# Beta's logarithm in the decay's bias, and the recurrence's dense products in one run of six, in the gated delta rule of a two-block model

## The chip, the cores and the metric

One core of one Trainium2 chip runs the whole program. The time is the device time of one execution in microseconds. The kernel before takes 2220.82 us (median of 3 runs, 2219.01 to 2222.67). The profiled execution took 2220.63 us.

## What the kernel computes

Two residual blocks run over 512 tokens of width 1024. The first has two layers: a gated delta rule mixer and a latent attention mixer, each followed by a SwiGLU. The second has a windowed attention and retention mixer, a convolution mixer and two cross attentions to a memory of 256 tokens. The change lies in the gated delta rule alone. Cut to what matters, for each of 8 heads (128 wide):

```python
beta = sigmoid(b_in);  g = -exp(a_log) * softplus(a_in + dt_bias)
kb = k * beta[..., None]
decay = exp(where(tril, g_cum_i - g_cum_j, -inf))
L = where(strict, einsum("id,jd->ij", kb, k) * decay, 0)
A = L + eye
u = triangular_solve(A, v * beta[..., None])
w = triangular_solve(A, kb * exp(g_cum)[..., None])
attn = einsum("id,jd->ij", q, k) * decay
# recurrence over the chunks:
v_new = u - w @ S
o = (q * exp(g_cum)) @ S + attn @ v_new
S = S * exp(g_last) + (k * exp(g_last - g_cum)).T @ v_new
```

followed by a norm of o, a gate silu(gate), and the output product with `gdn_w_out`.

## The kernel before, in words

**Engines.** The program is written by hand, one instruction list for each engine, and the engines meet in semaphores. SyncE (SP) loads the weights in slabs of 128 columns. GpSimd (POOL) splits each slab in two instructions into a high and a low part: `wH` (line 568) and `wL` (line 570). A split waits until the slab three places earlier has been used up (`slab_done`). TensorE (PE) forms each dense product as three products, high by high, high by low and low by high. ScalarE (ACT) does copies, exponentials and SiLU, and VectorE (DVE) the rest.

**A head.** The 8 heads of the delta rule run one after another in `head(i, ahead)` (PE line 924, ACT 1736, DVE 2337). Tokens are taken in four chunks of 128. While PE works on head i it also forms the four projections of head i+1 (key, query, value, gate: 96 dense products of 512 columns, `head_units`, line 826), dealt out in runs between the small products of head i: `dense(n)` issues the next n. In the last head, 7, there is no next head (`ahead` is false), and products of the memory's keys and values (`kv0`, `kv1`, 24 products of 256 columns to a slab) and of the output projection (`gdn_out`, `out_third`) take that place.

A head has three parts:

- *Opening.* ACT makes the logarithm and powers of the keys' squared norms (lines 1715 to 1718), squares the previous head's output (`head_squares`, line 1702) and exponentiates the decay with a bias for each key, `dec_bias` (line 1725). DVE adds the query norm's term to those squares (`head_sums`, line 2319), and PE sums them with a product by ones (line 922), whose result ACT turns into the norm (1707, 1709). PE forms the keys by (keys times beta) (line 939) and keys by queries (line 952). DVE multiplies the first by the decay (`LT`, line 2342) and starts the inverse of A in blocks of 64 (lines 2347 and 2350).
- *Inversion.* Five rounds of 64 by 64 products (line 901) with `dense(4)` between them. Each round passes through DVE.
- *Recurrence.* For each chunk t: values by inverse (line 1009), w by S (1013, which waits for the new state S), S by queries (1016), a dense run of four, the state's increment (1024) and the output (1025), a dense run of two. ACT copies `v_new` (1765). DVE updates S (2408, 2411), then filters a row of the next head's value (`conv`, 2291), then forms one row sum of the modulation weights (`ada_row`, 2082, 128x1024), which belongs to a later layer.

**Rows over tokens.** `head_rows` (line 840) spreads two rows of head i+1 over 128 partitions, each by one product from 64 partitions: the decay's sums behind t = 1, and beta behind t = 3. DVE multiplies the keys by the spread beta (`keys_by_beta`, line 2304), which the product of line 939 waits for. `key_factors` (2309 to 2313) makes the three small factors `dec_bias`, `kdec_by` and `v_by`.

## Time and profile before

| what | value |
|---|---|
| median of 3 runs | 2220.82 us |
| profiled execution, own time | 2220.63 us |
| its span | 2218.8 us |
| PE busy | 2151.1 us (97%) |
| DVE busy | 1152.6 us (52%) |
| ACT busy | 604.3 us (27%) |
| POOL busy | 1218.5 us (55%) |
| PE's share of the chain that ended last | 88% |

The 1.8 us between the span and the execution's own time lie around the first and the last instruction. The eight heads lie between about 75 and 450 us of the span. In the timeline a PE instruction's start is what counts: the products are pipelined, so that durations overlap, and a dense product of 512 columns starts some 0.23 us behind the one before it. A product in full fp32 is shown as two instructions (x2 for one product).

### The profile page before, as it was taken

To read this page: it belongs to the slowest core of one execution; us is meant where nothing else is said; L and a number is where in the kernel's file an instruction comes from. 1 tells how busy PE (TensorE), PEld (TensorE's weight loads), DVE (VectorE), ACT (ScalarE), POOL (GpSimd) and SP (SyncE) were. 2 spreads that over 40 slices of the span, in tenths; PEclk is the share of its full clock that TensorE was granted. 3 is DMA by queue.
4 is the path that set the end of the run, shared out by engine and by line. 5 is a ranking of instruction groups with operands and counts; after the bars stand their busy time and mean duration, and the time that the engine had idled before them with its cause. 6 is when DMAs were issued, how large, how long until landed. Compare 5 with 4: busy or idle time off the path is not lost.

```text
span 2218.8 us, 29386 instructions
## 1 busy us (share of the span) xinstructions
PE 2151.1 (97%) x11960; PEld 1716.1 (77%) x11960; DVE 1152.6 (52%) x1595; ACT 604.3 (27%) x1234; POOL 1218.5 (55%) x687
## 2 busy tenths in 40 slices
PE   7899999989999999999999999999999999999998
PEld 5677777778888887777788888777777878887886
DVE  4666666557457374554431322477764365346332
ACT  4434543332112023342320201422332230002113
POOL 5433333367778676333566666554445276657663
PEclk9999999999999999999999999999999999999999
DMA  8522322246465453111333333322224133333331
GB/s 272 174 75 88 105 68 87 77 143 207 144 199 180 152 185 106 58 52 49 114 101 99 95 95 94 97 80 73 67 58 123 39 114 98 96 91 95 105 105 66
DMA packets 366020, 239.88 MB, mean 108 GB/s; under 512 B 11352, under 2 KB 350654, under 8 KB 365759
## 3 DMA queue, kind: packets, MB, share of 16 engines
q1 hardware_dynamic: 364268, 234.07, 35.1%
q10 hardware_dynamic: 1618, 3.94, 0.5%
q8 instruction: 95, 1.56, 0.3%
q14 instruction: 39, 0.31, 0.0%
HBM read 233.79 MB, written 4.19 MB: 107 GB/s over the span
## 4 chain that ended last, share of the span: by engine, by line
PE 88%; DVE 5%; POOL 2%; ACT 2%; DMA 1%; issue 1%; SPq 1%; ACTq 0%; DVEq 0%; POOLq 0%
PE bank L611 16%; PE bank L613 16%; PE bank L612 16%; PE bank L835 8%; PE bank L630 3%; PE bank L632 3%; PE bank L631 3%; PE mid L901 2%; POOL wL L570 1%; PE mid L1408 1%; PE bank L647 1%; PE bank L649 1%; PE bank L648 1%; PE bank L868 1%; DVE WIDE L2082 1%
## 5 line engine op out<-in xcount | busy, mean ns | idle before, releaser
L568 POOL TENSOR_SCALAR wH<-stage 128x1024 fp32r<-128x1024 f32 (+1 forms) x340 | 387.3, 1139 | 944.8 <-PE bank L613 260.3
L570 POOL TENSOR_TENSOR wL<-stage,wH 128x1024 fp32r<-128x1024 f32 (+1 forms) x340 | 831.9, 2447 | 28.4
L611 PE MATMUL bank<-hH,wH 128*128 128x512 f32 x944 | 368.6, 390 | 0.7 <-DVE A L2159 0.3
L613 PE MATMUL bank<-hH,wL 128*128 128x512 f32 x944 | 367.4, 389 | 0.0
L612 PE MATMUL bank<-hL,wH 128*128 128x512 f32 x944 | 367.3, 389 | 0.0
L611 PE MATMUL bank<-RA,wH 128*128 128x512 f32 (+1 forms) x788 | 284.6, 361 | 7.6 <-DVE RA L2173 3.0
L612 PE MATMUL bank<-RA,wH 128*128 128x512 f32 (+1 forms) x788 | 282.4, 358 | 0.0
L613 PE MATMUL bank<-RA,wL 128*128 128x512 f32 (+1 forms) x788 | 282.3, 358 | 0.0
L611 PEld LDWEIGHTS bank<-hH,wH 128*128 128x128 f32 x944 | 177.2, 188 | 39.7 <-issue 3.3
L613 PEld LDWEIGHTS bank<-hH,wL 128*128 128x128 f32 x944 | 177.2, 188 | 37.0
L612 PEld LDWEIGHTS bank<-hL,wH 128*128 128x128 f32 x944 | 177.2, 188 | 36.7 <-issue 0.2
L611 PEld LDWEIGHTS bank<-RA,wH 128*128 128x128 f32 x788 | 150.0, 190 | 32.6 <-issue 5.2
L612 PEld LDWEIGHTS bank<-RA,wH 128*128 128x128 f32 x788 | 150.2, 191 | 21.8 <-issue 0.5
L613 PEld LDWEIGHTS bank<-RA,wL 128*128 128x128 f32 x788 | 150.2, 191 | 21.4
L2082 DVE CUSTOM_DVE_ANT_0 WIDE<-WIDE,cbc,vec 128x1024 f32<-128x1024 f32 x80 | 158.4, 2009 | 0.7 <-DMA WIDE<-in_ada_t 0.6
L1561 ACT ACTIVATE A<-bank 128x512 f32<-128x512 f32 (+1 forms) x85 | 47.0, 556 | 374.6 <-PE bank L613 354.5
L2142 DVE SCALAR_TENSOR_TENSOR xT<-bank,modT,xT 128x512 f32<-128x512 f32 x62 | 46.5, 751 | 177.9 <-PE bank L613 167.8
L630 PE MATMUL bank<-hH,wH 128*128 128x512 f32 x296 | 128.7, 435 | 6.4 <-POOL wL L570 6.1
L2211 DVE TENSOR_TENSOR A<-bank,A 128x512 f32<-128x512 f32 x44 | 30.4, 692 | 196.4 <-PE bank L613 190.8
L632 PE MATMUL bank<-hH,wL 128*128 128x512 f32 x296 | 116.6, 394 | 0.0
L631 PE MATMUL bank<-hL,wH 128*128 128x512 f32 x296 | 116.1, 392 | 0.0
L835 PE MATMUL bank<-hL,wH 128*128 128x512 f32 x248 | 108.0, 435 | 0.0
(418 smaller groups left out, 3526.5 us busy)
## 6 DMA issues: line engine op xcount, KB each, us to landing
WIDE<-in_ada_t SPq DMA_DIRECT2D x46, 1024.0 KB, 6.1
stage<-in_ffn_w_gate SPq DMA_DIRECT2D x44, 512.0 KB, 3.8
stage<-in_ffn_w_up SPq DMA_DIRECT2D x44, 512.0 KB, 3.8
stage<-in_c_wkv SPq DMA_DIRECT2D x32, 512.0 KB, 3.9
stage<-in_gdn_w_in SPq DMA_DIRECT2D x32, 512.0 KB, 4.1
stage<-in_ffn_w_down SPq DMA_DIRECT2D x32, 512.0 KB, 3.9
stage<-in_o_w_in SPq DMA_DIRECT2D x32, 512.0 KB, 4.0
stage<-in_e_w_in SPq DMA_DIRECT2D x26, 512.0 KB, 3.8
```

Of the source, the lines that this page charges most:

```text
L568: pool.tensor_scalar(high[:, 0:n], raw[:, 0:n], 1.0, 0.0, ALU.mult, ALU.add).then_inc(w_high, 1)
L570: pool.tensor_tensor(low[:, 0:n], raw[:, 0:n], high[:, 0:n].bitcast(F32), ALU.subtract).then_inc(w_split, 1)
L611: pe.matmul(bank[:, 0:n], h[:, k, c], xh[:, k, :], start=first and k == 0, stop=False)
L612: pe.matmul(bank[:, 0:n], h[:, k, c], xl[:, k, :], start=False, stop=False)
L613: mm = pe.matmul(bank[:, 0:n], l[:, k, c], xh[:, k, :], start=False, stop=last and k == kc - 1)
L630: pe.matmul(acc[j % 2][:], h, hH[:, k, :], start=k == 0, stop=False)
L631: pe.matmul(acc[j % 2][:], h, hL[:, k, :], start=False, stop=False)
L632: mm = pe.matmul(acc[j % 2][:], l, hH[:, k, :], start=False, stop=k == KD - 1)
L835: mm = pe.matmul(acc[j % 2][:], l if part == 2 else h, (hL if part == 1 else hH)[:, k, :], start=k == 0 and part == 0, stop=k == KD - 1 an ...
L1561: act.activation(out, acc[b][:, 0:n], func).then_inc(taken[b], 1)
L2082: ins = dve.tensor_tensor_reduce(out=w, in0=w, in1=c_bank if n < ADA_HEAD else cbc[:], scale=1.0, scalar=vec[:, at:at + 1], op0=ALU.mult, ...
L2142: dve.scalar_tensor_tensor(out=xT[:, k, :], in0=bank[:], scalar=gate[:, k:k + 1], in1=xT[:, k, :], op0=ALU.mult, op1=ALU.add).then_inc(tak ...
```

## The change

Beta leaves the rows. Its logarithm, minus ln(1 + exp(-b)), is taken up in `tok[:, 0]`, so that `dec_bias` carries it, and the decay that DVE multiplies by is already scaled by beta of the key's token. So one row instead of two is made and spread (`head_row`), `keys_by_beta` and `v_by` go, and the product of keys by keys needs the keys alone. It moves from the opening into the recurrence of the head before, at t = 1 (`keys_by_keys`). Keys by queries takes its place in the opening, goes to bank B5 instead of B4, and no longer waits for the norm of the head before. The product by ones follows it directly.

In the recurrence `dense(4)` and `dense(2)` become one `dense(6)` ahead of the wait for `v_new`, and the first `ada_row` of a head moves from behind the first state into the last round of the inversion. In the last head the 48 products of `kv1` are dealt out in runs of six beside the rounds (`beside`), the output projection follows later, and 12 products instead of 3 stand behind the product by ones of head 7.

**PE, recurrence, t = 1 into t = 2, head 1.** Before (L1016 is S by queries, L1024 and L1025 the increment and the output, L848 the spread row, L1009 and L1013 the next chunk's first two):

```order
L1016 MATMUL mid<-A,S 128x128
L835 MATMUL bank1<-hL,wH1 128x512
L835 MATMUL bank1<-hH,wL1 128x512
L835 MATMUL bank1<-hH,wH1 128x512
L835 MATMUL bank1<-hL,wH1 128x512
L1024 MATMUL mid<-A 128x128
L1025 MATMUL mid<-A 128x128
L835 MATMUL bank1<-hH,wL1 128x512
L835 MATMUL bank1<-hH,wH1 128x512
L848 MATMUL mid<-RA,pick 128x512
L1009 MATMUL mid<-A 128x128
L1013 MATMUL mid<-S,A 128x128
```

After (the same products are now L1037, L1049, L1050, L845 and L1030; L854 is keys by keys, and L834 the dense product):

```order
L1037 MATMUL mid<-A,S 128x128
L854 MATMUL mid<-A 128x128 x4
L834 MATMUL bank1<-hL,wH1 128x512
L834 MATMUL bank1<-hH,wL1 128x512
L834 MATMUL bank1<-hH,wH1 128x512
L834 MATMUL bank1<-hL,wH1 128x512
L834 MATMUL bank1<-hH,wL1 128x512
L834 MATMUL bank1<-hH,wH1 128x512
L1049 MATMUL mid<-A 128x128
L1050 MATMUL mid<-A 128x128
L845 MATMUL mid<-RA,pick 128x512
L1030 MATMUL mid<-A 128x128
```

Keys by keys stands ahead of the dense run, and the two runs are one: nothing dense is left between the increment and the next chunk.

**PE, opening of head 2.** Before (L939 is keys by beta's keys, L922 the product by ones, L952 keys by queries):

```order
L835 MATMUL bank0<-hL,wH2 128x512
L939 MATMUL mid<-A 128x128 x4
L835 MATMUL bank0<-hH,wL2 128x512
L835 MATMUL bank0<-hH,wH2 128x512
L922 MATMUL mid<-A,tab 128x512
L835 MATMUL bank0<-hL,wH2 128x512
L835 MATMUL bank0<-hH,wL2 128x512
L835 MATMUL bank0<-hH,wH2 128x512
L835 MATMUL bank0<-hL,wH2 128x512
L835 MATMUL bank0<-hH,wL2 128x512
L835 MATMUL bank0<-hH,wH2 128x512
L952 MATMUL mid<-A 128x128 x4
```

After (L968 is keys by queries, L942 the product by ones, L921 what L901 was):

```order
L834 MATMUL bank0<-hL,wH2 128x512
L968 MATMUL mid<-A 128x128 x4
L942 MATMUL mid<-A,tab 128x512
L834 MATMUL bank0<-hH,wL2 128x512
L834 MATMUL bank0<-hH,wH2 128x512
L834 MATMUL bank0<-hL,wH2 128x512
L834 MATMUL bank0<-hH,wL2 128x512
L834 MATMUL bank0<-hH,wH2 128x512
L834 MATMUL bank0<-hL,wH2 128x512
L834 MATMUL bank0<-hH,wL2 128x512
L834 MATMUL bank0<-hH,wH2 128x512
L921 MATMUL mid<-tab,inv 64x64 x8
```

The product by ones now stands eight dense products behind the head's start where it stood ten, and the 64 by 64 products follow its eight dense ones directly.

**DVE, end of head 2 and opening of head 3.** Before (L2298 is the decay's row, L2304 `keys_by_beta`, L2309 to L2313 `key_factors`, L2319 `head_sums`, L2342 the product that makes `LT`):

```order
L2291 SCALAR_TENSOR_TENSOR yt<-bank,cw,yt 128x509
L2082 ISA WIDE,modT<-WIDE,cbc,vec 128x1024
L2082 ISA modT 128x1
L2298 TENSOR_TENSOR A<-mid,tab 128x512
L2304 TENSOR_TENSOR A<-mid,A 128x512
L2309 SCALAR_TENSOR_TENSOR kn<-kn,tok 128x4
L2312 TENSOR_TENSOR kn<-kn,tok 128x4
L2313 TENSOR_TENSOR kn<-kn,tok 128x4
L2319 SCALAR_TENSOR_TENSOR A<-sq,A 128x512
L2342 TENSOR_TENSOR A<-mid,A 128x512
L2347 TENSOR_TENSOR inv<-A,tab 64x2x64 x4
```

After (L2326 is the decay's row, L2331 and L2334 `key_factors`, L2340 `head_sums`, L2363 makes `LT`):

```order
L2319 SCALAR_TENSOR_TENSOR yt<-bank,cw,yt 128x509
L2110 ISA WIDE,modT<-WIDE,cbc,vec 128x1024
L2110 ISA modT 128x1
L2326 TENSOR_TENSOR A<-mid,tab 128x512
L2331 SCALAR_TENSOR_TENSOR kn<-kn,tok 128x4
L2334 TENSOR_TENSOR kn<-kn,tok 128x4
L2340 SCALAR_TENSOR_TENSOR A<-sq,A 128x512
L2363 TENSOR_TENSOR A<-mid,A 128x512
L2368 TENSOR_TENSOR inv<-A,tab 64x2x64 x4
```

Two instructions are gone ahead of `head_sums`; the order of the rest stands.

The diff, without the declarations:

```diff
--- before.py
+++ after.py
...
@@ -815,9 +815,8 @@
                 pe.matmul(B4[:, 32:64], ones, gflat, start=True, stop=True).then_inc(g["gsum"], 1)
-                for bank, n, by in ((SS, 4, table("upto")), (B5, 1, ident)):
-                    for t in range(TT):
-                        mm = pe.matmul(bank[0:8, t * P:(t + 1) * P], tok[:, n, t, :], by, start=True, stop=True)
+                for t in range(TT):
+                    mm = pe.matmul(SS[0:8, t * P:(t + 1) * P], tok[:, 4, t, :], table("upto"), start=True, stop=True)
                 mm.then_inc(g["gsum"], 1)
@@ -837,16 +836,37 @@
 
-            def head_rows(i, n):
+            def head_row(i):
 
                 if i == 0:
-                    pe.wait_ge(g["rowlo"], 2)
-                elif n == 0:
+                    pe.wait_ge(g["rowlo"], 1)
+                else:
                     pe.wait_ge(g["p"], i * 6)
-                else:
-                    pe.wait_ge(g["s"], i * 3)
-                pe.matmul((SS, B5)[n][:], pick[0:64, i:i + 1].broadcast_to((64, P)), gate_row[:, n, :],
+                pe.matmul(SS[:], pick[0:64, i:i + 1].broadcast_to((64, P)), gate_row,
                           start=True, stop=True).then_inc(g["rows"], 1)
+
+            def keys_by_keys(i):
+
+                if i:
+                    pe.wait_ge(g["wt"], i)
+                for t in range(TT):
+                    c = slice(t * P, (t + 1) * P)
+                    mm = pe.matmul(B3[:, c], k_[:, c], k_[:, c], start=True, stop=True)
+                mm.then_inc(g["gram"], 1)
+
+            def kv_units(name, j, first, end):
+
+                s, uses = SLAB0[name] + j, USE0[name] // 2 + j // 2
+                for n in range(first, end):
+                    k, part = divmod(n, 3)
+                    if n == 0:
+                        pe.wait_ge(w_split, s + 1)
+                        free(j % 2, uses)
+                    h, l = (w[:, k, :] for w in halves(s))
+                    mm = pe.matmul(acc[j % 2][:, 0:MEM], l if part == 2 else h, (memL if part == 1 else memH)[:, k, :],
+                                   start=n == 0, stop=n == 3 * KD - 1)
+                    if n == 3 * KD - 1:
+                        mm.then_inc(slab_done, 1)
 
@@ -925,6 +945,13 @@
 
+                def beside(n):
+
+                    if n < 8:
+                        kv_units("kv1", n // 4, n % 4 * 6, n % 4 * 6 + 6)
+                    else:
+                        gdn_out((n - 8) // 2, (n % 2,))
+
                 def dense(n):
@@ -932,40 +959,32 @@
                 if not ahead:
-                    kv_slabs("kv0", (0,))
-                pe.wait_ge(g["kb"], i + 1)
+                    kv_units("kv0", 0, 0, 3 * KD)
+                pe.wait_ge(g["silu"], i * 3 + 2)
+                if i:
+                    pe.wait_ge(g["s"], i * 3)
                 for t in range(TT):
                     c = slice(t * P, (t + 1) * P)
-                    mm = pe.matmul(B3[:, c], k_[:, c], Pm[:, c], start=True, stop=True)
+                    mm = pe.matmul(B5[:, c], k_[:, c], q[:, c], start=True, stop=True)
                 mm.then_inc(g["gram"], 1)
-                at = dense(2)
                 if i:
                     head_squares(i - 1)
-                at = dense(6)
+                at = dense(8)
                 if not ahead:
-                    kv_slabs("kv0", (1,))
-                pe.wait_ge(g["silu"], i * 3 + 2)
-                if i:
-                    pe.wait_ge(g["ors"], i)
-                for t in range(TT):
-                    c = slice(t * P, (t + 1) * P)
-                    mm = pe.matmul(B4[:, c], k_[:, c], q[:, c], start=True, stop=True)
-                mm.then_inc(g["gram"], 1)
-                if not ahead:
-                    kv_slabs("kv1", (0,))
+                    kv_units("kv0", 1, 0, 3 * KD)
 
...
                 if not ahead:
-                    kv_slabs("kv1", (1,))
+                    beside(0)
                 for n in range(1, 6):
...
                     if not ahead:
-                        gdn_out(n - 1, (0,))
+                        beside(2 * n - 1)
                     if n == 1 and i:
@@ -978,7 +997,7 @@
                     if not ahead:
-                        gdn_out(n - 1, (1,))
+                        beside(2 * n)
 
@@ -986,7 +1005,8 @@
                 if not ahead:
-                    gdn_out(5)
+                    gdn_out(1, (1,))
+                    gdn_out(2, (0,))
                 pe.wait_ge(g["p"], i * 6 + 6)
@@ -994,7 +1014,8 @@
                 if not ahead:
-                    gdn_out(6)
+                    gdn_out(2, (1,))
+                    gdn_out(3)
 
@@ -1014,22 +1035,23 @@
                         pe.matmul(B6[:, c], S[:, t % 2, :], E[:, c], start=True, stop=False)
+                        if ahead and t == 1:
+                            keys_by_keys(i + 1)
                     elif ahead:
                         keys_turn(i + 1)
-                    at = dense(4)
-                    if not ahead:
-                        out_third("gdn_out", t, t, t + 1)
+                    at = dense(6)
+                    if not ahead and t < TT - 1:
+                        gdn_out(4 + t)
+                    elif not ahead:
+                        out_third("gdn_out", 0, 0, 1)
                     pe.wait_ge(g["vn"], i * 4 + t + 1)
...
                         mm.then_inc(g["o_ps"], 1)
-                    at = dense(2)
                     if ahead and t == 1:
-                        head_rows(i + 1, 0)
-                    if ahead and t == TT - 1:
-                        head_rows(i + 1, 1)
+                        head_row(i + 1)
                 at = dense(2)
@@ -1038,15 +1060,16 @@
             keys_turn(0)
-            head_rows(0, 0)
-            head_rows(0, 1)
+            head_row(0)
+            keys_by_keys(0)
             for i in range(0, 7):
...
             head(7, False)
-            for k in range(4, 6):
+            for k in range(1, 3):
                 out_third("gdn_out", k, k, k + 1)
             head_squares(7)
-            out_third("gdn_out", 6, 6, 7)
+            for k in range(3, 7):
+                out_third("gdn_out", k, k, k + 1)
             gdn_out(7)
@@ -1719,7 +1742,7 @@
                 act.wait_ge(g["dec"], i + 1)
-                act.wait_ge(g["kds"], 3 * i + 1)
+                act.wait_ge(g["kds"], 2 * i + 1)
                 for t in range(TT):
@@ -1729,8 +1752,9 @@
                 copy_sum(1, SLAB0["gdn"] + i * 4 + 3, gs[i % 2])
-                act.wait_ge(g["kds"], 3 * i + 3)
+                act.wait_ge(g["kds"], 2 * i + 2)
                 scaled_tiles(kdec, B7, lambda t: kdec_by[:, t:t + 1]).then_inc(g["tok"], 1)
+                act.wait_ge(g["gexp"], 2)
                 scaled_tiles(ktok, B7, lambda t: tok[:, 2, t, i:i + 1]).then_inc(g["tok"], 1)
@@ -1742,16 +1766,19 @@
                     head_sum(i + 1, 0)
-                else:
-                    kv_copies(1)
                 if i:
...
                 act.activation(gs[i % 2], gs[i % 2], ACT.Silu).then_inc(g["gs"], 1)
+                if not ahead:
+                    kv_copies(1, (0,))
                 act.wait_ge(g["vtr"], i + 1)
-                scaled_tiles(v, B7, lambda t: v_by[:, t:t + 1]).then_inc(g["v"], 1)
+                act.wait_ge(g["rk"], 3 * i + 3)
+                scaled_tiles(v, B7, lambda t: k_norm[:, t:t + 1]).then_inc(g["v"], 1)
+                if not ahead:
+                    kv_copies(1, (1,))
                 if ahead:
@@ -1777,6 +1804,8 @@
             act.activation(tmp8[:, 0], tmp8[:, 3], ACT.Exp, scale=-1.0).then_inc(g["eb"], 1)
+            act.wait_ge(g["eb"], 1)
+            own(act.activation(tmp8[:, 3], tmp8[:, 0], ACT.Ln, bias=1.0))
             act.wait_ge(par_in, 64)
@@ -1786,13 +1815,12 @@
             gc = B4[:, 0:32].rearrange("p (t h) -> p t h", h=8)
-            act.activation(tmp8[:, 0], gc, ACT.Exp).then_inc(g["gexp"], 1)
+            act.activation(tok[:, 2], gc, ACT.Exp).then_inc(g["gexp"], 1)
             act.wait_ge(g["zab"], 2)
...
             act.wait_ge(g["pick"], 1)
-            for n, bank in enumerate((SS, B5)):
-                act.activation(gate_row[0:8, n, :], bank[0:8, :], ACT.Copy).then_inc(g["rowhi"], 1)
+            act.activation(gate_row[0:8, :], SS[0:8, :], ACT.Copy).then_inc(g["rowhi"], 1)
             act.preload_act_table_set(SILU)
@@ -2294,23 +2322,16 @@
 
-                dve.wait_ge(g["rows"], i * 2 + 1)
+                dve.wait_ge(g["rows"], i + 1)
                 dve.tensor_tensor(tiles(decs[i % 2]), tiles(SS[:]), on_tiles(table("decay_neg")), ALU.add).then_inc(g["dec"], 1)
-
-            def keys_by_beta(i):
-
-                dve.wait_ge(g["rows"], i * 2 + 2)
-                dve.wait_ge(g["silu"], i * 3 + 1)
-                dve.tensor_tensor(Pm, B5[:], k_, ALU.mult).then_inc(g["kb"], 1)
 
...
                                          op0=ALU.mult, op1=ALU.subtract).then_inc(g["kds"], 1)
-                dve.wait_ge(g["rk"], 3 * i + 3)
+                dve.wait_ge(g["rk"], 3 * i + 2)
                 dve.tensor_tensor(kdec_by, k_inv2, tok[:, 3, :, i], ALU.mult).then_inc(g["kds"], 1)
-                dve.tensor_tensor(v_by, k_norm, tok[:, 1, :, i], ALU.mult).then_inc(g["kds"], 1)
 
@@ -2351,7 +2372,7 @@
                 dve.wait_ge(g["gram"], i * 2 + 2)
-                own(dve.tensor_tensor(attn, B4[:], dec, ALU.mult))
+                own(dve.tensor_tensor(attn, B5[:], dec, ALU.mult))
                 own.settle()
@@ -2395,6 +2416,7 @@
                         dve.sem_inc(g["xt"], 1)
+                        ada_row(3 * i)
                     below(n)
@@ -2413,10 +2435,10 @@
                         conv(i + 1, 2, (2 - t,))
-                    ada_row(3 * i + t)
+                    if t:
+                        ada_row(3 * i + t)
                 if ahead:
                     decay_rows(i + 1)
-                    keys_by_beta(i + 1)
                     key_factors(i + 1)
@@ -2454,18 +2476,17 @@
                .then_inc(g["zab"], 2)
+            dve.wait_ge(g["zab"], 2)
+            own(dve.tensor_tensor(tok[:, 0], tok[:, 0], tmp8[:, 3], ALU.add))
             dve.wait_ge(g["gexp"], 2)
-            own(dve.tensor_tensor(tok[:, 2], tok[:, 1], tmp8[:, 0], ALU.mult))
+            own(dve.tensor_tensor(tok[:, 3], tok[:, 3], tok[:, 1], ALU.mult))
             dve.wait_ge(kv_out, 16 * 2)
...
             own.settle()
-            for n, bank in enumerate((SS, B5)):
-                dve.wait_ge(g["rowhi"], n + 1)
-                dve.tensor_tensor(gate_row[32:40, n, :], bank[0:8, :], gate_row[0:8, n, :].bitcast(F32), ALU.subtract)\
-                   .then_inc(g["rowlo"], 1)
+            dve.wait_ge(g["rowhi"], 1)
+            dve.tensor_tensor(gate_row[32:40, :], SS[0:8, :], gate_row[0:8, :].bitcast(F32), ALU.subtract).then_inc(g["rowlo"], 1)
             conv(0, 2, (2, 1, 0))
             decay_rows(0)
-            keys_by_beta(0)
             key_factors(0)
...
                 head(i, True)
```

## Rows read from the trace of the kernel before

**Rows 1.** Windows view: us, busy us of PE, PEld, DVE, ACT, POOL, clock, DMA share, GB/s.
```profile
75.00:450.00 375.00, 365.51 (x3602) 278.56 (x3600) 237.65 (x455) 160.39 (x421) 129.05 (x72) 1.00 0.29 86
...
403.50:407.00 3.50, 3.50 (x17) 3.50 (x18) 2.28 (x5) 2.19 (x9) 1.05 (x1) 0.52 0.54 159
```

**Rows 2.** Timeline, PE, head 3's recurrence: start us, us, engine line op, tiles, count.
```profile
260.41 0.40 PE L835 MATMUL bank<-hH,wH 128*128 128x512 f32 x1
...
261.16 0.49 PE L1009 MATMUL mid<-A 128*128 128x128 f32 x2
262.10 0.46 PE L1013 MATMUL mid<-S,A 128*128 128x128 f32 x2 [0.45 <-DVE S L2411]
```

**Rows 3.** Timeline, DVE, end of the inversion and the recurrence, head 3.
```profile
253.36 0.42 DVE L2400 TENSOR_SCALAR A<-mid 64x256 f32<-64x256 f32 x1 [1.70 <-PE mid L993]
...
258.51 3.18 DVE L2082 CUSTOM_DVE_ANT_0 WIDE<-WIDE,cbc,vec 128x1024 f32<-128x1024 f32 x1
```

**Rows 4.** Timeline, POOL, a split behind head 3's opening, and one in its recurrence.
```profile
225.16 1.05 POOL L568 TENSOR_SCALAR wH<-stage 128x1024 fp32r<-128x1024 f32 x1 [7.55 <-PE bank L835]
226.29 2.83 POOL L570 TENSOR_TENSOR wL<-stage,wH 128x1024 fp32r<-128x1024 f32 x1
...
258.22 2.38 POOL L570 TENSOR_TENSOR wL<-stage,wH 128x1024 fp32r<-128x1024 f32 x1
```

**Rows 5.** Timeline, PE, from the end of head 2 through the opening of head 3.
```profile
221.68 0.39 PE L1013 MATMUL mid<-S,A 128*128 128x128 f32 x2
...
223.51 0.40 PE L835 MATMUL bank<-hH,wH 128*128 128x512 f32 x1
...
224.60 0.40 PE L835 MATMUL bank<-hH,wL 128*128 128x512 f32 x1
...
226.43 0.39 PE L835 MATMUL bank<-hL,wH 128*128 128x512 f32 x1
...
227.78 0.40 PE L835 MATMUL bank<-hH,wH 128*128 128x512 f32 x1
228.02 1.02 PE L922 MATMUL mid<-A,tab 128*128 128x512 f32 x2
...
230.03 0.39 PE L835 MATMUL bank<-hH,wH 128*128 128x512 f32 x1
230.48 1.13 PE L952 MATMUL mid<-A 128*128 128x128 f32 x8
...
233.52 0.46 PE L901 MATMUL mid<-inv,A 64*64 64x64 f32 x16
```

**Rows 6.** Timeline, ACT, opening of head 3.
```profile
225.17 0.58 ACT L1702 ACTIVATE A<-mid 128x512 f32<-128x512 f32 x1
...
229.07 0.60 ACT L1707 ACTIVATE A<-mid 128x512 f32<-128x512 f32 x1 [1.20 <-PE mid L922]
...
232.71 0.44 ACT L1742 ACTIVATE inv<-mid 128x256 f32<-128x256 f32 x1
```

**Rows 7.** Timeline, DVE, opening of head 3.
```profile
225.30 0.92 DVE L2312 TENSOR_TENSOR kn<-kn,tok 128x4 f32<-128x4 f32 x1 [0.16 <-ACT kn L1718]
...
226.22 0.68 DVE L2319 SCALAR_TENSOR_TENSOR A<-sq,A 128x512 f32<-128x512 f32 x1
```

**Rows 8.** Timeline, PE, last head.
```profile
403.49 0.40 PE L611 MATMUL bank<-RA,wH 128*128 128x256 f32 x1 [1.92 <-ACT A L1561]
...
442.09 0.39 PE L1009 MATMUL mid<-A 128*128 128x128 f32 x2
442.56 0.46 PE L1013 MATMUL mid<-S,A 128*128 128x128 f32 x2
...
445.58 1.13 PE L922 MATMUL mid<-A,tab 128*128 128x512 f32 x2
...
451.02 0.50 PE L868 MATMUL bank<-RA,wH 128*128 128x512 f32 x1 [3.63 <-DVE RA L2164]
```

**Rows 9.** Timeline, PE, the gates ahead of head 0.
```profile
83.95 1.91 PE L820 MATMUL mid<-tab,tok 128*8 128x128 f32 x16
```

## What the change was expected to do, before it was run

> **What bounds the kernel now.** The windows view comes first. Between 75 and 450 us, where the eight heads lie, PE is busy for 365.5 of 375 us, DVE for 238 and ACT for 160 [rows 1]. Then the list of who waited for whom, which gives PE few waits there, and the timeline of PE, read by starts: one head's pattern returns in the others, so one head stands for all. Two places matter: the recurrence, where one wait per head is left [rows 2], and the opening, where PE, ACT and DVE are close together [rows 5 to 7]. All times below are offsets from the start of the last w by S of a head (L1013 at 221.68), unless they are clock times.
>
> **Prices of PE's products.** Eight dense products take 226.43 - 224.60 = 1.83, so 0.229 each. From 226.43 to 227.78 stand two dense intervals and the four products L939: 1.35 - 0.46 = 0.89 for the four, 0.22 each. From 223.51 to 224.60 stand two dense intervals and the spread of beta's row: 1.09 - 0.46 = 0.63 [rows 5]. So joining dense runs gives nothing by itself: four small products between dense ones cost what four small products cost. What the longer runs move is where PE waits.
>
> **Gates, ahead of head 0.** Eight products of 8 rows take 1.91 [rows 9]; four go: -0.9. ACT's new logarithm and DVE's sums are of 32 columns and far ahead of their readers. Head 0's opening waits on ACT and DVE, so its spread row gives nothing.
>
> **Recurrence, heads 0 to 6.** Keys by keys adds 0.89. The wait for S goes at t = 2: L1009 to L1013 take 262.10 - 261.16 = 0.94 against 0.22, which is 0.72, with 0.07 for the slower start behind a wait [rows 2]. It came from DVE's `ada_row`, which stood 3.18 and ended at 261.69, 1.09 behind the POOL instruction that ended at 260.60 [rows 3, 4]; the state waited behind it. It is now moved to the inversion. Its work beyond standing still is 261.69 - 260.60 = 1.1 or a little more, and in the inversion it meets an idle gap of DVE of 1.70 ahead of L2400 [rows 3], so I cost it at nothing; late, it would cost up to 0.3. Its weights' semaphore is reached earlier, and SP's next load with it, which harms nothing, since those weights were loaded a head ahead. With no dense run between the increment and w by S, two chunks now wait for S, behind t = 0 and t = 2. The last head has that order already: 442.56 - 442.09 = 0.47 against 0.22 [rows 8]; with the slower start 0.3 each, 0.6. Behind t = 1 the spread row covers it. That row stands next to small products now: -0.1. Sum: +0.89 + 0.6 - 0.79 - 0.1 = **+0.6 per head, +4.2 for seven**. Bounds: +0.3 if S comes in time once, +0.9 if `ada_row` is late.
>
> **Opening, heads 1 to 6, PE alone.** Beta's row goes (0.63), keys by beta's keys goes (0.89), and so does the wait of L952 for the norm: 230.48 - 230.03 = 0.45 against 0.23, 0.22 [rows 5]. That is 1.74 off 233.52 - 221.68 = 11.84. But the product by ones is moved up. It stood at 228.02 - 221.68 = 6.34. Without the row (0.63) and with two dense products fewer before it (0.46) PE arrives at 5.25, and with 0.07 from the wait for S, which shifts all engines here alike, at 5.3. It needs DVE's `head_sums`, which needs ACT's squares, done at 225.17 + 0.58, 4.07 (4.14 shifted) [rows 6].
>
> **The step that decides.** POOL's split of the head's fourth slab starts 0.56 behind the slab's last product (224.60 to 225.16) [rows 4, 5]. That product was at 2.92. It now comes at 1.83 + 0.46 = 2.29, 2.36 shifted, since beta's row no longer stands before it. So L568 runs from 2.92 to 3.97 and L570 can start at 4.05, some 0.13 before ACT's squares let `head_sums` start (4.18). In the kernel before it was the other way: L2312 stood still behind L568 for 0.92, a 4-column instruction, `head_sums` followed at 226.22, 0.07 ahead of L570's 226.29, and it was L570 that came out long, 2.83 against 2.38 elsewhere [rows 4, 7]. `ada_row` shows what the other order costs: started 0.29 behind an L570 it ended 1.09 behind that one's end [rows 3, 4]. So rows say that a DVE instruction with both inputs in SBUF stands still until the POOL instruction ends. `head_sums` is one. It would end at 4.05 + 2.38 + 0.6 = 7.0 instead of 4.9, and PE, there at 5.3, waits some 1.7.
>
> The Trainium skill, "SBUF — State Buffer", section "SBUF: two separate sides", states the rule: the port pair is an exclusive lock, and whichever of the two starts first has it for its whole instruction. The trace agrees (3.18 and 0.92 above). By that rule 0.13 us of lead are enough, and the sum is the one that follows; without it, the other rival's.
>
> **The opening then.** L922 starts at 7.04. PE alone would reach the first inversion product at 7.04 + (11.84 - 6.34) - 0.89 - 0.22 + 0.46 = 11.9. ACT is later: 1.05 from L922 to L1707 and 3.64 from there to the copy L1742, which takes 0.44 [rows 5, 6]: 12.17, with the start of PE 12.26. Against 11.84: **+0.4 per head, +2.5 for six**. DVE's `LT` is also queued behind `head_sums`, but ends its chain before PE asks.
>
> **Last head.** The spread row's 0.63 is lost to the same wait. Keys by beta's keys is off PE (-0.9; its counterpart is in the recurrence above). Nine of the products stand behind the product by ones now: 9 x 0.229 = -2.1. The wait of 1.92 for a bank ahead of `kv0`'s second slab stays [rows 8], since it hangs on the same norm, and so does the half clock behind it (0.52 granted, the level of 1.2 GHz, [rows 1]), 17 products at 0.21 instead of 0.12. Sum -3.0. From there to the last y the chain is ACT's and DVE's, 451.02 - 445.58 = 5.44 [rows 8], unchanged; PE had 3.63 idle in it and now has the nine products, which is the 2.1 counted. With the shorter gap the clock may stay up behind it, 0.35 to the next slab. Bounds: -1.5 if DVE's norm stands behind a POOL split in round 1, -4 if not at all.
>
> **Sum.** -0.9 + 4.2 + 2.5 - 3.0 - 0.35 = +2.4 on the profiled execution's 2220.63, which is 0.2 under the median: **2223**.
>
> **The rivals.**
>
> *A. `head_sums` gets through first.* Then L570 waits and PE does not. Squares by ones start at 5.3. L1707 follows at 6.35 and the copy ends at 6.35 + 3.64 + 0.44 = 10.4; PE alone would be at 5.3 + 4.85 = 10.15, so the copy decides, and with PE's start behind a wait it is 10.6. That is -1.2 per head, -7.1 for six, and the last head gives -3.8: -0.9 + 4.2 - 7.1 - 3.8 - 0.35 = -8, **2213**. For it: the lead of L570 is 0.13 by sums of rows, and the start of a record need not be the moment of the lock. Against it: L2319 won by 0.07 before, so records this close have told the order rightly.
>
> *B. The new gap brings PE's clock down.* PE stands still some 1.7 us in each opening. The gap of 1.92 at 403.49 was followed by 3.5 us at a granted 0.52 [rows 8, 1]; the eight dense products behind the wait would take 0.2 more each, 1.6 a head. Six heads: +10, **2233**, slower. Against it: this gap is 0.2 shorter, and it has full runs of products on both sides. [...]
>
> *C. Nothing of it:* the recurrence comes out at +0.3 and the opening at 0, the last head at -3: -2, **2219**.
>
> **How the numbers follow.** My forecast 0.56, A 0.30, B 0.08, C 0.06. The difference that a measurement of this kernel tells from none is about 0.2%, 4.4 us. The forecast, with its parts' bounds about 3 us to each side, gives slower 0.13, same 0.39, faster 0.04; A faster 0.27, same 0.03; B slower; C same 0.04, faster 0.02. Together faster 0.33, same 0.46, slower 0.21. The range reaches to A below, 2212, and above to the forecast with its late bounds, 2227; B is left out. The forecast's own range is 2219 to 2227.
>
> **What the profile after would show.** `head_sums` (L2340) some 2.8 us long in heads 1 to 6, the product by ones (L942) behind a wait for it of about 1.7, L570 at 2.4 there and not 2.83: the forecast. `head_sums` at 0.68, L570 long, PE waiting a little for the copy of the inverse: A. A granted clock under 1 between 130 and 400 us: B. L1034 waiting for S twice a head, 0.25 each, and no DVE instruction of 3.18 any more: the recurrence. In the last head, a gap before the last y of some 1.6 instead of 3.63. The prediction is wrong if `ada_row` holds up line 2422 in the inversion, or if a head's length changes by more than 1.5 us either way.

## The result: slower by 0.2%, and where the profile after has it

The kernel after takes 2225.54 us (median of 10 runs, 2220.85 to 2231.3), the kernel before 2221.06 in the same rounds (10 runs, 2218.29 to 2223.85). The ratio is 1.0022, 95% interval 1.0014 to 1.0031. In a second set of rounds, below, it was 1.0014 (1.0005 to 1.0023). The forecast was 2223 in 2212 to 2227. The profiled execution took 2225.12, span 2223.3.

First the windows of the kernel after, as [rows 1]: the heads, and the stretch behind the wait for a bank in the last head (columns: us, busy us of PE, PEld, DVE, ACT, POOL, granted clock, DMA share, GB/s).

```profile
75.00:450.00 375.00, 358.89 (x3574) 277.24 (x3573) 227.28 (x437) 159.08 (x419) 125.79 (x72) 1.00 0.29 86
409.78:413.20 3.42, 3.42 (x17) 3.42 (x18) 2.04 (x6) 2.19 (x9) 0.22 (x1) 0.56 0.59 180
```

PE is busy for 358.9 us where it was 365.5, and yet the heads end no earlier: what left PE is there again as standing still. The list of waits of PE between 70 and 450 us says for whom (us in total, times, longest):

```profile
PE mid L942 <- DVE A L2340: 9.7, 7, 1.5
PE mid L921 <- ACT inv L1766: 2.1, 6, 0.3
PE bank L866 <- ACT A L1584: 1.9, 1, 1.9
PE mid L921 <- DVE inv L2371: 1.1, 1, 1.1
PE mid L921 <- DVE inv L2406: 0.2, 1, 0.2
```

The product by ones (L942, L922 before) waits in seven openings for DVE's sum (L2340, L2319 before). All eight executions of that sum, after and before (shortest, median and longest in ns), and then POOL and DVE in one opening, to be held against [rows 4, 7]; the last w by S of the head before starts at 267.25.

```profile
L2340 DVE SCALAR_TENSOR_TENSOR A<-sq,A x8: 693/2784/2792, 139.0 to 447.7; 128x512 f32<-128x512 f32 x8
```

```profile
L2319 DVE SCALAR_TENSOR_TENSOR A<-sq,A x8: 676/680/693, 140.2 to 444.8; 128x512 f32<-128x512 f32 x8
```

```profile
270.17 1.05 POOL L568 TENSOR_SCALAR wH<-stage 128x1024 fp32r<-128x1024 f32 x1 [7.70 <-PE bank L834]
271.31 2.36 POOL L570 TENSOR_TENSOR wL<-stage,wH 128x1024 fp32r<-128x1024 f32 x1
```

```profile
271.43 2.79 DVE L2340 SCALAR_TENSOR_TENSOR A<-sq,A 128x512 f32<-128x512 f32 x1
274.14 0.68 DVE L2363 TENSOR_TENSOR A<-mid,A 128x512 f32<-128x512 f32 x1
```

L570 starts 0.12 ahead of the sum, at 4.06 and 4.18 of the opening. The sum has 2.79 in its record and ends 0.55 behind L570. The last of the eight, at 447.7 behind head 7, runs while POOL is idle, and takes 0.69. L570 itself is 2.36 long, where it was 2.83. PE and ACT in the same opening, to be held against [rows 5, 6], and the recurrence before it, against [rows 2]:

```profile
260.01 0.39 PE L1030 MATMUL mid<-A 128*128 128x128 f32 x2
260.42 0.46 PE L1034 MATMUL mid<-S,A 128*128 128x128 f32 x2
260.94 1.06 PE L854 MATMUL mid<-A 128*128 128x128 f32 x8
...
264.18 0.49 PE L1030 MATMUL mid<-A 128*128 128x128 f32 x2
264.50 0.39 PE L1034 MATMUL mid<-S,A 128*128 128x128 f32 x2
...
266.78 0.39 PE L1030 MATMUL mid<-A 128*128 128x128 f32 x2
267.25 0.46 PE L1034 MATMUL mid<-S,A 128*128 128x128 f32 x2
...
271.69 1.05 PE L968 MATMUL mid<-A 128*128 128x128 f32 x8
274.27 1.13 PE L942 MATMUL mid<-A,tab 128*128 128x512 f32 x2 [1.53 <-DVE A L2340]
...
277.16 0.46 PE L921 MATMUL mid<-tab,inv 64*64 64x64 f32 x16
279.57 0.46 PE L921 MATMUL mid<-inv,A 64*64 64x64 f32 x16 [0.35 <-ACT inv L1766]
```

```profile
275.43 0.60 ACT L1730 ACTIVATE A<-mid 128x512 f32<-128x512 f32 x1 [1.87 <-PE mid L942]
...
279.07 0.44 ACT L1766 ACTIVATE inv<-mid 128x256 f32<-128x256 f32 x1
```

In the recurrence the wait of 0.72 at t = 2 is gone (0.32 between L1030 and L1034), and two of 0.2 have come, at t = 1 and t = 3 (0.41 and 0.47 between the two lines, 0.22 without a wait). In the opening PE is at the product by ones at 5.5 and starts it at 7.02; the first inversion product is at 12.32, against 11.84. A head takes 44.1 us in place of 43.0.

Ada's sum in its new place, the last round of the inversion (DVE):

```profile
253.75 1.28 DVE L2110 CUSTOM_DVE_ANT_0 WIDE<-WIDE,cbc,vec 128x1024 f32<-128x1024 f32 x1 [0.19 <-DVE A L2415]
254.96 0.08 DVE L2110 DVE_READ_ACCUMULATOR2_ANT modT<- 128x1 f32 x1
255.25 0.42 DVE L2422 TENSOR_SCALAR A<-mid 64x256 f32<-64x256 f32 x1 [0.21 <-PE mid L1013]
```

It takes 1.28, and L2422 behind it waits 0.21 for PE and not for the sum. So neither of the prediction's two signs of being wrong came: L2422 is not held up, and a head's length moved by 1.1 us, not by more than 1.5.

### The profile page after: what moved, and what is told of

Its sections match the earlier page's. It is cut to its first block, busy times and chain, and to the rows that moved or that the text cites. A ratio compares the mean times of both kernels' runs of the same rounds, so it can differ in the third digit from the quotient of the medians.

```text
span 2223.3 us, 29338 instructions
## 1 busy us (share of the span) xinstructions
PE 2147.5 (97%) x11944; PEld 1717.3 (77%) x11944; DVE 1144.2 (51%) x1579; ACT 604.2 (27%) x1234; POOL 1212.9 (55%) x687
## 3 DMA queue, kind: packets, MB, share of 16 engines
q8 instruction: 95, 1.56, 0.3%
## 4 chain that ended last, share of the span: by engine, by line
PE 87%; DVE 4%; ACT 4%; POOL 2%; DMA 1%; issue 1%; SPq 1%; ACTq 0%; DVEq 0%; POOLq 0%
PE bank L611 16%; PE bank L613 16%; PE bank L612 15%; PE bank L834 6%; PE bank L630 3%; PE bank L632 3%; PE bank L631 3%; PE mid L921 2%; PE mid L1431 1%; POOL wL L570 1%; PE bank L647 1%; PE bank L648 1%; PE bank L649 1%; PE bank L888 1%; PE mid L655 1%; DVE A L2340 1%
## 5 line engine op out<-in xcount | busy, mean ns | idle before, releaser
L568 POOL TENSOR_SCALAR wH<-stage 128x1024 fp32r<-128x1024 f32 (+1 forms) x340 | 384.3, 1130 | 955.6 <-PE bank L613 258.9
L570 POOL TENSOR_TENSOR wL<-stage,wH 128x1024 fp32r<-128x1024 f32 (+1 forms) x340 | 829.3, 2439 | 28.4
L611 PE MATMUL bank<-RA,wH 128*128 128x512 f32 (+1 forms) x756 | 274.8, 363 | 6.8 <-DVE RA L2201 3.0
L613 PE MATMUL bank<-RA,wL 128*128 128x512 f32 (+1 forms) x756 | 272.9, 361 | 0.0
L612 PE MATMUL bank<-RA,wH 128*128 128x512 f32 (+1 forms) x756 | 272.8, 361 | 0.0
L611 PEld LDWEIGHTS bank<-RA,wH 128*128 128x128 f32 x756 | 143.3, 190 | 30.4 <-POOL wL L570 3.5
L612 PEld LDWEIGHTS bank<-RA,wH 128*128 128x128 f32 x756 | 143.4, 190 | 21.7 <-issue 0.5
L613 PEld LDWEIGHTS bank<-RA,wL 128*128 128x128 f32 x756 | 143.4, 190 | 21.4
L2110 DVE CUSTOM_DVE_ANT_0 WIDE<-WIDE,cbc,vec 128x1024 f32<-128x1024 f32 x80 | 145.7, 1852 | 1.6 <-DVE A L2415 1.5
L834 PE MATMUL bank<-hL,wH 128*128 128x512 f32 x248 | 105.5, 425 | 0.0
```

Source lines behind the costliest of these rows:

```text
L568: pool.tensor_scalar(high[:, 0:n], raw[:, 0:n], 1.0, 0.0, ALU.mult, ALU.add).then_inc(w_high, 1)
L570: pool.tensor_tensor(low[:, 0:n], raw[:, 0:n], high[:, 0:n].bitcast(F32), ALU.subtract).then_inc(w_split, 1)
L611: pe.matmul(bank[:, 0:n], h[:, k, c], xh[:, k, :], start=first and k == 0, stop=False)
L612: pe.matmul(bank[:, 0:n], h[:, k, c], xl[:, k, :], start=False, stop=False)
L613: mm = pe.matmul(bank[:, 0:n], l[:, k, c], xh[:, k, :], start=False, stop=last and k == kc - 1)
L834: mm = pe.matmul(acc[j % 2][:], l if part == 2 else h, (hL if part == 1 else hH)[:, k, :], start=k == 0 and part == 0, stop=k == KD - 1 an ...
```

## The experiments

Times are medians; "before" is the kernel before in the same rounds. Offsets count from the last w by S. In e1, e5, e6 and e9 POOL's second instruction is line 573, and lines behind it have moved by a few. Two measures stand beside each other: the medians, and a head's length, the distance between the last w by S of two heads in a row, in the profile.

The medians carry something that is not the edit. Each timed execution has its mean granted clock on record. In the kernel before it is 0.9922 on average in the rounds with e1 to e4 (25 executions), 0.9911 in those with e5 to e8 (16) and 0.9923 in those with e9 and e10 (21); within each of these sets an execution with 0.001 more is some 1.5 us shorter. e5, e7 and e9 have 0.9944 to 0.9950. So up to 5 or 6 us of a difference of medians can go with the clock (an estimate from these numbers). Whether an edit has a part in that is open.

**e1.** POOL made to wait, to give DVE the first turn.

```diff
                 pool.wait_ge(w_high, s + 1)
+                h, j = divmod(s - SLAB0["gdn"], 4)
+                if j == 2 and 2 <= h <= 8:
+                    pool.wait_ge(g["osum"], h - 1)
                 pool.tensor_tensor(low[:, 0:n], raw[:, 0:n], high[:, 0:n].bitcast(F32), ALU.subtract).then_inc(w_split, 1)
```

> The kernel after, with one wait added: in each opening POOL's L570 (the second half of its split) starts only when DVE's sum for the previous head (L2340) is done. Theory (POOL, 0.12 us ahead, holds DVE's sum for 2.1 us, and PE behind it): the sum takes 0.69 and not 2.79, the product by ones starts without its 1.53 us wait, L570 starts at 4.9 us of the opening in place of 4.06. Then DVE's L2368 (both inputs in SBUF) can stand behind L570 in turn until 7.3, so the first inversion product comes 1.35 us earlier, not 1.7: six openings 8.1, and 0.5 in the last head: 8.6 under the kernel after, 2217. Rival (the sum is slow for another reason, or the inversion is bound by ACT's chain anyway): within 2 us of the kernel after, 2224 to 2226. Either way the half-clock stretches behind 900 us may come or go: 1 to 2 us each.

Measured: 2216.8 against 2222.5 of before, ratio 0.9978 (0.9968 to 0.9988). DVE in one opening (last w by S at 221.13), and PE's wait:

```profile
225.32 0.69 DVE L2343 SCALAR_TENSOR_TENSOR A<-sq,A 128x512 f32<-128x512 f32 x1
226.52 0.69 DVE L2366 TENSOR_TENSOR A<-mid,A 128x512 f32<-128x512 f32 x1 [0.51 <-ACT A L1751]
227.25 2.39 DVE L2371 TENSOR_TENSOR inv<-A,tab 64x128 f32<-64x128 f32 x4
```

```profile
226.16 2.38 POOL L573 TENSOR_TENSOR wL<-stage,wH 128x1024 fp32r<-128x1024 f32 x1 [1.05 <-DVE A L2343]
```

```profile
PE mid L924 <- DVE inv L2374: 4.9, 6, 0.8
```

The sum is 0.69 long, the wait for it is gone, and the first inversion product is at 11.01, 1.31 earlier. POOL's instruction now holds the four that start the inverse (2.39, 1.24 without it). L2366, with one operand in PSUM, stands inside the same L573 and keeps its 0.69. Both parts of the expectation came: the sum is free, and the start of the inverse is the next to be held. The time itself is in part luck: in this profile the half clock behind the wait for a bank in the last head is missing too (granted 1.00 behind the same wait of 1.93), which is worth some 1.7 us and was not in the expectation.

**e5.** The same wait, moved on to the start of the inverse.

```diff
-                    pool.wait_ge(g["osum"], h - 1)
+                    pool.wait_ge(g["xt"], (h - 1) * 7 + 1)
```

> As e1_pool_waits, but L570 waits until DVE has also made the start of the inverse (L2371). In e1 the sum was 0.69 long and the time 2216.8, and DVE's L2368, both inputs in SBUF, was the next to stand: 2.39 against 1.24, with PE waiting 0.81 for what follows it. Theory (same lock, second victim): L2368 back at 1.24, PE's 0.81 gone; the first inversion product moves from 11.01 to about 10.55 of the opening, where ACT's copy of the inverse holds it. 0.46 in each of six heads, 2.8: 2214. Rival (L570, now 3 us later than in the kernel after, is missed by PE or stands in the way of a DVE instruction behind it): 2217 or more.

Measured: 2210.72 against 2223.35, 0.9941 (0.9929 to 0.9954). DVE in an opening:

```profile
223.94 1.24 DVE L2371 TENSOR_TENSOR inv<-A,tab 64x128 f32<-64x128 f32 x4
```

A head is 42.36 long, 0.48 under e1, and the first inversion product is at 10.53. That is the expected step. The median is 3 us lower than expected: its profile has none of the half-clock stretches near 920 us that the profiles of e1 and of the kernel after have (below), and its executions have the highest granted clock of all, 0.9950 on average.

**e10.** No wait, only another order of PE: the keys by queries go ahead of the last two dense products of the slab.

```diff
@@ in the opening
                     kv_units("kv0", 0, 0, 3 * KD)
-                pe.wait_ge(g["silu"], i * 3 + 2)
-                if i:
-                    pe.wait_ge(g["s"], i * 3)
-                for t in range(TT):
-                    c = slice(t * P, (t + 1) * P)
-                    mm = pe.matmul(B5[:, c], k_[:, c], q[:, c], start=True, stop=True)
-                mm.then_inc(g["gram"], 1)
+                if i == 0:
+                    queries(0)
@@ behind the recurrence (queries holds the lines above)
+                if ahead:
+                    queries(i + 1)
                 at = dense(2)
```

> The kernel after, with the eight products keys by queries put ahead of the two dense products that end the slab, 0.9 us of PE in front of the slab's last product; nothing waits that did not, and PE's work is the same. Theory (0.12 us of lead decides): POOL's L568 comes at 3.8 in place of 2.92, L570 is ready at 4.95, and DVE's sum, ready at 4.18, stands behind L568 alone and is done by 5.6, so the product by ones comes at 5.6 in place of 7.02. L570 then ends near 7.95 and holds DVE's L2368 in turn, so the first inversion product gains 0.8, not 1.4: six openings 4.8, last head 0.5: 5 under the kernel after in the same rounds. Rival (the kernel after is slow for the work it moved, not for this order): no change, or slower where the longer stretch between the chunks is missed.

Measured: 2218.0 against 2221.76, 0.9985 (0.9976 to 0.9994); the kernel after had 2224.57 in these rounds. DVE, then POOL, in one opening (221.28):

```profile
225.46 1.22 DVE L2347 SCALAR_TENSOR_TENSOR A<-sq,A 128x512 f32<-128x512 f32 x1 [0.41 <-ACT A L1732]
226.62 0.69 DVE L2370 TENSOR_TENSOR A<-mid,A 128x512 f32<-128x512 f32 x1
227.35 2.68 DVE L2375 TENSOR_TENSOR inv<-A,tab 64x128 f32<-64x128 f32 x4
```

```profile
225.09 1.06 POOL L568 TENSOR_SCALAR wH<-stage 128x1024 fp32r<-128x1024 f32 x1 [8.59 <-PE bank L834]
226.23 2.70 POOL L570 TENSOR_TENSOR wL<-stage,wH 128x1024 fp32r<-128x1024 f32 x1
```

The sum stands behind L568 for 0.5, then goes ahead of L570, whose record is now the long one. With PE's work the same, a head is 43.06 in place of 44.14: the order of the two instructions alone is worth 1.1 us a head, a little more than the 0.8 expected.

**e2.** The sum brought forward instead.

```diff
@@ ACT (the old call, three lines further down, goes)
+                if i:
+                    head_squares(i - 1)
                 act.activation(k_log, k_sum, ACT.Ln, bias=EPS).then_inc(g["rk"], 1)
@@ DVE
                 if ahead:
                     decay_rows(i + 1)
-                    key_factors(i + 1)
                 head_sums(i)
+                if ahead:
+                    key_factors(i + 1)
```

> The kernel after, with ACT's squares of the head's result ahead of its three small instructions on the keys' norm (0.45 us earlier), and DVE's sum ahead of its two small instructions for the factors. No wait is added. Theory: the sum now stands behind L568 alone (to 3.97 us of the opening) and is next when that ends, so it goes ahead of L570 and takes 0.7 to 0.95; L570 is late by 0.6. The price: the exponentials of the decay (L1748) start 0.7 later, at 4.8, so ACT's chain gives back part. First inversion product 1.1 us earlier than in the kernel after; six openings 6.6, last head 0.5: 2218. Rival (the order of two records 0.1 apart does not decide, POOL has the port whenever it asks): the sum stays at 2.3 or more and the time is 2225 or, with the later exponentials, 2228.

Measured: 2234.66 against 2222.53, 1.0057 (1.0044 to 1.0069). Neither theory had that. DVE, then ACT, then POOL, in one opening (272.79):

```profile
276.55 0.76 DVE L2340 SCALAR_TENSOR_TENSOR A<-sq,A 128x512 f32<-128x512 f32 x1 [1.44 <-ACT A L1725]
277.23 2.32 DVE L2331 SCALAR_TENSOR_TENSOR kn<-kn,tok 128x4 f32<-128x4 f32 x1
```

```profile
279.65 1.28 ACT L1748 ACTIVATE A<-A,kn 128x128 f32<-128x128 f32 x4 [2.70 <-DVE kn L2334]
```

```profile
276.85 2.67 POOL L570 TENSOR_TENSOR wL<-stage,wH 128x1024 fp32r<-128x1024 f32 x1
```

The sum did go first, and has 0.76 in its record. But behind it stood L2331, `dec_bias`, four elements to a partition: with both tensors in SBUF it was held by L570, and its record is 2.32 us long (0.16 in the kernel before). ACT's exponentials of the decay wait for it, then the inverse, for which PE waits 2.4 us in each of the six openings. My expectation had charged 0.7 for those two small instructions, as if only the large one could be held.

A second thing came with it. Two heads, one after the other, in the windows view:

```profile
135.86:180.83 44.97, 42.00 (x430) 32.01 (x430) 27.71 (x54) 19.31 (x51) 14.13 (x8) 1.00 0.26 83
180.83:226.87 46.04, 43.30 (x429) 32.67 (x430) 27.12 (x54) 19.31 (x51) 14.13 (x8) 0.96 0.28 82
```

In four of the six heads (the second, third, fifth and sixth of them) the granted clock is 0.96: behind the wait of 2.4 us stands a stretch of some 3.4 us at half clock. These heads are 45.8 to 46.0 long, the two without it 44.95 and 44.97, against 44.14 in the kernel after. So the held instruction costs 0.8 a head more than the kernel after, and the half clock another 0.9 in four heads. That is the mechanism of rival B, with a longer wait than the kernel after has.

**e3.** The runs of six split into four and two again.

```diff
-                    at = dense(6)
+                    at = dense(4)
...
                         mm.then_inc(g["o_ps"], 1)
+                    at = dense(2)
                     if ahead and t == 1:
```

> The kernel after, with the run of six dense products of each chunk of the recurrence split again into four and two, as before the change. Theory: w by S waits for the state 0.22 less behind t = 0 and 0.25 less behind t = 2, so 0.45 to 0.5 per head, 3.5 in seven: 2222. The opening does not move: L570 still 0.1 ahead of DVE's sum, 2.79 us long, since the slab's last product stays where it was. Rival (the run of six is what pays for the new place of keys by keys): the vn product waits more for t = 1 and 3, and the head is no shorter: 2225.5.

Measured: 2221.63 against 2222.53, 0.9998 (0.999 to 1.0007). L1030 to L1034 is 0.22 again at t = 1 and t = 3, a head is 43.61, 0.53 shorter, and the opening is unchanged (the sum 2.79, the first inversion product at 12.27). So the run of six costs 0.53 a head, 3.7 in all; that is read from the heads, since the kernel after was not in these rounds.

**e8 and e4.** Ada's sum put back in the kernel after, as the diff shows, and moved alone in the kernel before, by the same lines with the signs turned round.

```diff
                         dve.sem_inc(g["xt"], 1)
-                        ada_row(3 * i)
...
-                    if t:
-                        ada_row(3 * i + t)
+                    ada_row(3 * i + t)
```

> The kernel after, with the sum of ada's row put back behind the state's first chunk, where it stood before the change. Theory: keys by keys (0.9 of PE) now stands between that state and the product that waits for it, and the late state was 0.72 late without it, so it is covered: no change, 2225.5. Rival (the two are additive, as the prediction summed them): 0.5 or more a head longer, 2229 and up.

> The kernel before, with one part of the change alone: of the three sums of ada's rows, the one behind the state's first chunk is moved into the inversion. Theory: the wait of 0.72 for the state at t = 2 goes, 0.79 with the slower start, in seven heads; the sum meets an idle stretch of DVE there. 5.5 under the kernel before: 2215.5. The opening stays in its old order (the sum 0.07 ahead of L570). Rival: the row's sum holds up what comes behind it in the inversion by up to 0.5 per head, and 2 are left: 2219.

Measured: e8 2223.72 against 2223.35, 1.0001 (0.9993 to 1.001); e4 2218.13 against 2222.53, 0.9979 (0.997 to 0.9988). In e8 the sum is held again, and nothing comes of it:

```profile
260.68 2.71 DVE L2110 CUSTOM_DVE_ANT_0 WIDE<-WIDE,cbc,vec 128x1024 f32<-128x1024 f32 x1
```

A head is 44.13 with it and 44.14 without it. That e8 is level with the kernel before in its rounds, and the kernel after is not in its own, is no gain of e8: e8 had a granted clock of 0.9937 on average there, the kernel before 0.9911. In e4 a head is 42.33 in place of 43.0, 0.67 less. So moving the sum is worth 0.67 a head where nothing else stands at t = 1, and nothing once keys by keys stand there. Both expectations held, though e4's median gained 4.4 us where 5.5 were expected.

**e7.** The kernel before with the last head's order of the kernel after: all lines of the change under `if not ahead` on PE and ACT, with `kv_units` and `beside`, and those behind `head(7, False)`. The core of it:

```diff
-                    kv_slabs("kv1", (1,))
+                    beside(0)
...
-                        out_third("gdn_out", t, t, t + 1)
+                    if not ahead and t < TT - 1:
+                        gdn_out(4 + t)
...
-            for k in range(4, 6):
+            for k in range(1, 3):
                 out_third("gdn_out", k, k, k + 1)
             head_squares(7)
-            out_third("gdn_out", 6, 6, 7)
+            for k in range(3, 7):
+                out_third("gdn_out", k, k, k + 1)
```

> The kernel before, with the last head's dense products alone put in the order of the kernel after (kv1 in pieces in the inversion, gdn_out's k 4 to 6 in the recurrence, nine products behind the last product by ones). Theory: the nine products fill the gap ahead of the last y (3.63 to about 1.6), 2.1, and with the clock's half stretch behind that gap 0.35: 2.5 less up to 460 us, 2220 against 2222.5. In the profiles of the kernel after and of e1 and e3, which all have this last head, two half-clock stretches near 921 and 1071 us cost 2.3 us more than in the profiles with the old one. If they hang on the new last head, they are here too and the time is that of the kernel before, 2222.5; if they are chance, they are not tied to it.

Measured: 2216.99 against 2223.35, 0.997 (0.9958 to 0.9981), 6.4 us where 2.5 were expected. The surplus goes with the clock: 0.9947 on average against 0.9911, which at 1.5 us for 0.001 is some 5 us (an estimate), so the medians do not size the edit. The profile does better. The windows view behind the wait for a bank (1.93), to be held against the second of [rows 1]:

```profile
404.29:407.80 3.51, 3.51 (x30) 3.51 (x31) 2.28 (x5) 2.57 (x10) 1.31 (x2) 1.00 0.48 140
```

Up to POOL's split at 456 us the gain is 4.5 over the start of the heads. 30 products stand in 3.5 us where 17 did: the half clock did not come behind that wait in this execution, which is 1.7 of it. The remaining 2.8 are near the 2.5 expected. The half clock is missing in the same place in the profiles of e1, e6 and e10, and there in those of before, after, the repeat, e3, e4, e5, e8 and e9, behind a wait of 1.92 or 1.93 us each time. So it is not tied to the last head's order, and what decides is open. The further half clock near 921 and 1071 us, for which e7 was also run, is not in its profile (granted 1.00 and 0.91, as in the kernel before): the new last head alone does not bring it.

**e6 and e9.** e6 is e5 with e3's edit. e9 is e6 with:

```diff
-                act.wait_ge(g["gexp"], 2)
-                scaled_tiles(ktok, B7, lambda t: tok[:, 2, t, i:i + 1]).then_inc(g["tok"], 1)
...
                 act.activation(by_parity(Xs), two_banks(0), ACT.Copy).then_inc(g["x"], 1)
+                act.wait_ge(g["gexp"], 2)
+                scaled_tiles(ktok, B7, lambda t: tok[:, 2, t, i:i + 1]).then_inc(g["tok"], 1)
```

> e5_pool_waits_inverse with the runs of e3_four_two (four and two dense products in each chunk of the recurrence). Theory: the two places are independent, 0.53 a head less, 3.7 under e5: 2210 to 2211. Rival (the recurrence's gain is lost because ACT's copy of the inverse sets the opening): 2214.

> e6_both, with ACT's second set of scaled tiles (ktok, 1.17) behind its copy of the inverse in place of ahead of it. In e6 that copy is what PE waits for in each opening, 0.35. Theory: it now comes 1.0 earlier, and the first inversion product goes from 10.45 to 10.05 to 10.1 of the opening, PE's own time: 0.4 in six heads, 2.4: 2207.5. Rival (what ACT does behind the copy, the silu of the gate and the values, is late by 1.2 in its place): the gain is lost there, 2210.

Measured: e6 2209.84 against 2223.35, 0.9938 (0.9924 to 0.9951); a head 41.80, 0.56 under e5. The medians of e5 and e6 are only 0.9 apart where the heads say 3.9; e6's granted clock was the lower one, 0.9934 against 0.9950. e9 2204.91 against 2221.76, 0.9928 (0.9916 to 0.9941); a head 41.39, the first inversion product at 10.04 and no wait of PE left in the openings of heads 1 to 6. e9's median is 16.9 us under the kernel before and 19.7 under the kernel after, the clock's part included.

**The kernel after again.**

> The kernel after, unchanged, in the same rounds as the two others and the kernel before. In the profiled executions it is 2.5 us behind the kernel before from 456 us on and 4.8 behind it from 1095 us on, where half-clock stretches at 921 us and 1071 us lie that the kernel before does not have; the kernel with ada's sum put back runs the same to 0.04 us up to 884 us and lacks the first of them. If they are chance, this profile may have other ones, and the difference over the rounds is 2.5 to 3 us, 1.0012. If they belong to the kernel after, they are at the same places again, and the difference is 4.5, 1.002.

Measured: 2224.57 (11 runs, 2223.12 to 2227.39) against 2221.76, 1.0014 (1.0005 to 1.0023). In the profile after, POOL's splits stand 2.5 behind those of before from 456 to 884 us, 4.05 at 922 and 4.84 from 1093 on, and no instruction was changed there. Between 915 and 935 us the windows view has, for the kernel after and for e8, whose work is the same in that place and 0.04 us apart in time at 884 us:

```profile
915.00:935.00 20.00, 18.06 (x81) 12.76 (x80) 9.28 (x18) 6.71 (x21) 7.58 (x6) 0.91 0.17 51
```

```profile
915.00:935.00 20.00, 18.06 (x85) 12.07 (x84) 10.81 (x21) 6.69 (x21) 7.59 (x6) 1.00 0.18 57
```

Both have the same busy time of PE; one shows the half clock for part of it. The profile of the repeat has it there again, and so have e1, e3 and e10; those of before, e2, e4 and e5 to e9 have not. The same five profiles have a granted 0.83 between 1060 and 1080 us, where the kernel before and e8 have 0.91. So these 1.6 us are not tied to the moved instructions, but they are not shown to be pure chance either: what decides is open. 2.3 of the 4.5 us between the two profiled executions are such stretches.

The expectation joined "at the same places again" with a difference of 4.5; the places came again, and the difference was 2.8. The clocks on record explain it in part. In these rounds the kernel after had 0.9935 on average (11 executions), the kernel before 0.9923 (21), and the profiled execution of the repeat was the longest of the eleven, 2227.39. With some 1.6 us for 0.001, the kernel after was helped by about 1.9 us; at the same clock the two would be some 4.7 apart (an estimate). So the 2.8 does not show that the difference is only the 2.5 of the heads.

## Why the prediction was right, step by step

- **The step that decides: right.** L570 at 4.06 (forecast 4.05), the sum at 4.18 (4.18), the product by ones at 7.02 (7.04), the sum 2.79 long (2.8). Without the held sum the product starts at 5.33 (e1), where the forecast had PE at 5.3. The order rested on a lead of 0.13 us worked out from rows, with a chance of 0.30 given to the other order: that it held was a close call, what follows from it was not. e1 and e10 show the cause: with the order turned round, by a wait or by PE's order, it is 0.69 and 1.22. The page "SBUF — State Buffer" of the Trainium skill, section "SBUF: two separate sides", states that whichever of the two starts first has the shared port pair for its whole instruction. The trace agrees at a lead of 0.12 us.
- **Opening:** forecast +0.4, measured +0.48. PE waits 0.35 for ACT's copy of the inverse; e9 shows that this wait, too, is an order on ACT.
- **Recurrence:** forecast +0.6, measured 9.72 against 9.02, +0.70. The two waits for S are 0.2 each; e3 gives 0.53 for them and what they delay. One term was booked wrongly though the sum came out: I took -0.79 for ada's sum and +0.89 for keys by keys as two edits. e8 shows that keys by keys alone cover the late state. In this kernel the move of ada's sum is worth nothing.
- **Gates:** forecast -0.9; from the products of 8 rows (L819, L820 before) to the turning of the keys (L655) there are 9.95 us for 10.82, -0.87.
- **Last head:** forecast -3.0, measured 48.71 against 51.94, -3.23. The half clock behind the wait for a bank came (0.56 granted), as forecast; with eight of twelve profiles having it, that was partly luck, worth 1.7. **Tail:** PE's gap ahead of the last y is 1.56 for 3.63, and the clock stays up behind it: 4.65 us to the next slab for 5.02, -0.37 for the -0.35 forecast. In the profile of the repeat the half clock comes one wait later instead, at 458 us behind a wait of 2.32 for POOL, and costs 1.5.
- **Sum:** forecast +2.4; 2.48 measured at 458 us. It holds -0.6 which the profile after already has ahead of the gates (L810, the first small products of the gates, starts at 76.27 against 76.88), so the change itself is about +3.1: 0.7 x 7 + 0.48 x 6 - 0.87 - 3.23 - 0.35 = +3.3, nearly.
- **Not foreseen:** the further 2.3 of half clock behind 900 us in the profiled execution. The median of the first rounds lies 2.5 over the forecast, and the slower side, to which I gave 0.21, came nearer than I thought. Since the clock alone moves a median by as much as the whole forecast difference, that the time fell within the range is the weaker evidence; the parts above are the stronger.
- **Rival A** had its price too high: it took -1.2 against the kernel before for the opening, and e1, which is that case, has 11.01 against 11.84, -0.8 (e10 -0.6). Its time was 2213; e1 and e10 took 2216.8 and 2218.0. It missed that L570, once it is late, holds the start of the inverse. Its sum also has a slip: six times its own 10.6 - 11.84 is -7.4, not -7.1. Rivals B and C fell. PE's 1.53 us of standing still brought no half clock in heads 1 to 6 (1.00 granted over the heads), nor did such a wait in any of the six openings of the repeat, e3 and e8; behind 2.4 us it came four times in six (e2). Between the two the length does not settle it, as the wait for a bank shows. And the openings did not come out at 0.

## What to carry to other kernels

Where POOL and DVE both read two tensors in SBUF, look for the pairs of their instructions whose starts are within a few tenths of each other, and ask which will be first after the edit. Work taken off one engine moves another's start across such an edge: here 0.6 us less of PE ahead of the end of a slab made DVE 2.1 us late. The cure is to let the long instruction that nobody waits for start last, by a wait or by an order, and to follow the queue to the next victim, small instructions included. And an edit is worth what it is worth beside the others: ada's sum was worth 0.67 a head alone and nothing here. Size such an edit by the part of the timeline that it touches; a median of the whole kernel also holds half-clock stretches of some 1.7 us each, some of them elsewhere.

## What the runs showed of the hardware that was not expected

- A held instruction was long whatever its size: four elements to a partition took 2.32 us (e2, 0.16 in the kernel before), 512 took 2.79 (0.68 before).
- DVE, when it already stands behind L568, goes ahead of L570, which follows 0.08 later: L570's record then grows from 2.36 to 2.70 (e10).
- A DVE instruction with one operand in PSUM keeps its 0.69 inside a POOL split of 2.38 (e1).
- The same wait of 1.92 to 1.93 us in the last head was followed by 3.4 us at a granted 0.52 or 0.56 in the kernels before and after, and by 1.00 in e1, e6, e7 and e10.
